# Issuing weight loads from ScalarE in a mixer, and adding half of the experts' rows in the last chunk

## The reference

```python
for l in range(DEPTH):                                   # 2 layers
    sh1, sc1, gt1, sh2, sc2, gt2 = modulation(cond, w_ada[l], b_ada[l])   # cond @ w_ada (1024 x 6144)
    h   = adaln(x, norm_attn[l], sh1, sc1)
    mix = mixer(h)      # windowed attention | bidirectional gated DeltaNet, then one output projection
    x   = residual(x, gt1, mix)
    x   = residual(x, gt2, routed_moe(adaln(x, norm_ffn[l], sh2, sc2)))   # 16 experts, 2 per token
```

## Time and profile before

| | us |
|---|---|
| median of 3 runs | 1897.55 |
| lowest, highest | 1893.96, 1897.66 |
| the profiled execution, its own time | 1897.15 |
| its span, first to last instruction | 1895.4 |
| PE busy | 1631.1 (86%) |
| DVE, ACT, POOL busy | 1207.6, 932.4, 242.2 |
| mean granted clock of TensorE | 0.932 |

### The profile page before, as it was taken

The page is one execution under the profiler, slowest core; times in us unless marked ns, Lnnn a source line. Parts: engine busy times, 40 slices in busy tenths (PEclk is TensorE's granted clock), DMA queues, the critical chain, the costliest instruction groups (busy, mean ns, idle before and its releaser), DMA issues. The chain is left out here.

```text
span 1895.4 us, 32729 instructions
## 1 busy us (share of the span) xinstructions
PE 1631.1 (86%) x11909; PEld 1325.4 (70%) x11910; DVE 1207.6 (64%) x1728; ACT 932.4 (49%) x1438; POOL 242.2 (13%) x361
## 2 busy tenths in 40 slices
PE   3998886799895999999949989789979679999992
PEld 0798675687553888888838986678855468888881
DVE  1478453556346996996664883646654579899664
ACT  2254642233323886886543445323341278888651
POOL 0000035111000111111020000541200011111112
PEclk7899998999896999999969999879999889999996
DMA  8241356654305997997553110665331489999754
GB/s 339 78 151 48 100 153 163 189 178 143 137 34 205 412 405 294 380 408 269 211 218 112 56 48 1 174 197 157 95 129 53 167 304 402 408 397 409 296 198 178
DMA packets 186803, 392.96 MB, mean 207 GB/s; under 512 B 88682, under 2 KB 106114, under 8 KB 161094
## 3 DMA queue, kind: packets, MB, share of 16 engines
q1 hardware_dynamic: 163374, 326.12, 47.7%
q10 hardware_dynamic: 14824, 34.39, 4.6%
q0 software_dynamic: 8496, 30.94, 4.3%
HBM read 345.95 MB, written 45.45 MB: 207 GB/s over the span
## 5 line engine op out<-in xcount | busy, mean ns | idle before, releaser
L2363 DVE TENSOR_TENSOR expert_w_lo<-shared,expert_w_hi 128x2048 fp32r<-128x2048 f32 x192 | 433.4, 2287 | 58.3 <-ACT expert_w_hi L2302 58.3
L2302 ACT ACTIVATE expert_w_hi<-shared 128x2048 fp32r<-128x2048 f32 x192 | 366.5, 1913 | 44.1 <-PEq L146 39.6
L2229 PE MATMUL ps<-expert_w_hi,expert_x_hi 128*128 128x512 f32 x592 | 245.2, 414 | 11.0 <-DVE expert_x_lo L2358 9.2
L2231 PE MATMUL ps<-expert_w_hi,expert_x_lo 128*128 128x512 f32 x592 | 233.2, 394 | 0.0
L2230 PE MATMUL ps<-expert_w_lo,expert_x_hi 128*128 128x512 f32 x592 | 233.1, 394 | 0.0
L2229 PEld LDWEIGHTS ps<-expert_w_hi,expert_x_hi 128*128 128x128 f32 x592 | 113.5, 192 | 42.5 <-issue 12.9
L2231 PEld LDWEIGHTS ps<-expert_w_hi,expert_x_lo 128*128 128x128 f32 x592 | 112.3, 190 | 24.3
L2230 PEld LDWEIGHTS ps<-expert_w_lo,expert_x_hi 128*128 128x128 f32 x592 | 112.8, 191 | 18.7
L2284 PE MATMUL ps<-expert_w_hi,expert_hid_hi 128*128 128x512 f32 x296 | 115.8, 391 | 0.5 <-ACT expert_hid_hi L2337 0.5
L2199 POOL COPY expert_cur_idx<-slot_tokens 128x1 int32 x37 | 48.4, 1307 | 530.2 <-PE ps L2216 530.2
L2285 PE MATMUL ps<-expert_w_lo,expert_hid_hi 128*128 128x512 f32 x296 | 115.3, 390 | 0.0
(11 more groups left out here) (380 smaller groups left out, 3376.7 us busy)
## 6 DMA issues: line engine op xcount, KB each, us to landing
shared<-in_w_up SPq DMA_DIRECT2D x64, 1024.0 KB, 7.4
shared<-in_w_down SPq DMA_DIRECT2D x64, 1024.0 KB, 9.4
shared<-in_w_gate SPq DMA_DIRECT2D x64, 1024.0 KB, 8.3
qkv<-in_w_ada SPq DMA_DIRECT2D x20, 1280.0 KB, 6.1
shared<-in_w_in SPq DMA_DIRECT2D x10, 2048.0 KB, 9.2
y_table<-expert_y ACTq DMA_DIRECT2D x37, 512.0 KB, 8.5
qkvT<-in_w_ada SPq DMA_DIRECT2D x20, 768.0 KB, 8.5
setup_ada_ring<-in_w_ada SPq DMA_DIRECT2D x8, 1024.0 KB, 12.2
```

Of the source, the lines that this page charges most:

```text
L2229: pe.matmul(bank, x_hi[:, at], w_hi[:, j, w], start=(q == 0), stop=False)
L2231: return pe.matmul(bank, x_lo[:, at], w_hi[:, j, w], start=False, stop=(q == KD - 1))
L2302: act.activation(w_hi[:, j, :], raw[:, j, :], ACT.Copy).then_inc(w_hi_done, 1)
L2363: dve.tensor_tensor(w_lo[:, j, :], raw[:, j, :], w_hi[:, j, :].bitcast(F32), ALU.subtract).then_inc(w_lo_done, 1)
```

## The change

Three things change.

- `load_after` moves from SP's order to ACT's: it now stands behind the two exponentials of a pair (`exps`). The wait for `done` and both issues of the load move with it. With it goes the place of `scatter(0)`, `x_load(0)` and `y_load(0)`, which now stand ahead of `base_load(3)`.
- The tables are laid out anew. `base_x` and `base_y` are written in the order in which steps read them, so that a step loads X and Y in 2 DMAs each of 128 KB, not 4 of 64 KB. The corner and the scores' tables get one entry for each tile and direction, and a step loads each in one DMA, not two. Each corner store writes two entries of 64 rows.
- The rows of slot 0 are gathered and added in the last chunk of the experts' phase (`FirstHalf`): in layer 0 for tiles 0 and 1 (into piece 5 of the weights' raw buffer), in the last layer gathered for all five tiles and added for tiles 0 and 1; tiles 2 to 4 are added at the head of `combine_phase`. POOL starts these gathers once the last piece is split and all y stores but the last have landed. `Joined` gathers for tiles 0 and 1 only slot 1, and ACT does nothing for them. The gate row is now loaded ahead of `load_first`.

```diff
+EARLY = 2
@@ Joined
-            for n in range(2):
+            for n in range(int(t < EARLY), 2):
...
+        if t < EARLY:
+            dve.wait_ge(self.got[t], 16)
+            dve.scalar_tensor_tensor(out=b, in0=b, scalar=w, in1=g, op0=ALU.mult, op1=ALU.mult).then_inc(self.gated, 1)
+        else:
...
+class FirstHalf:
+    def gathers(self, pool):
+        for t in self.tiles:
+            pool.indirect_dma_start(out=self.rows[:, t, :], out_offset=None, in_=self.A.y_table,
+                                    in_offset=bass.IndirectOffsetOnAxis(ap=self.R.slots[:, 0, t:t + 1], axis=0)).then_inc(self.got[t], 16)
+
+    def dve_sum(self, dve, t):
+        G, a = self.G, self.rows[:, t, :]
+        dve.wait_ge(self.got[t], 16)
+        dve.scalar_tensor_tensor(out=a, in0=a, scalar=self.R.gates[:, 0, t:t + 1], in1=G.gate_view[:, int(t > 0), :],
+                                 op0=ALU.mult, op1=ALU.mult).then_inc(self.scaled, 1)
+        dve.wait_ge(self.scaled, t + 1)
+        dve.tensor_tensor(G.x[:, t, :], G.x[:, t, :], a, ALU.add).then_inc(self.summed, 1)
@@ projection_phase, ACT
-                    for t in range(2):
-                        joined.act_first(act, t)
@@ mixer_phase, SP
-                        sp.dma_start(A.corner[i], flat(BtLF[i])).then_inc(s_["bl_out"], 16)
+                        sp.dma_start(mine(A.corner, i, HB * DH * HB).rearrange("f (r n) -> f r n", r=HB), flat(BtLF[i])).then_inc(s_["bl_out"], 16)
...
-                    for d in range(2):
-                        sp.dma_start(flat(BtL)[half(d)], A.corner[place(s, d), half(d)]).then_inc(s_["bl_in"], 16)
+                    sp.dma_start(flat(BtL), both(A.corner, s, HB * DH * HB).rearrange("f (r n) -> f r n", r=HB)).then_inc(s_["bl_in"], 16)
...
-                    for d in range(2):
-                        for b in range(2):
-                            sp.dma_start(X[half(b), d], large(A.base_x, place(s, d), b)[:, d * DH:(d + 1) * DH]).then_inc(s_["xy_in"], 16)
+                    for b in range(2):
+                        sp.dma_start(eight_of(X, b), large(entry(A.base_x, 2 * s, 2), b)).then_inc(s_["xy_in"], 16)
...
                     if i + 1 < FRONT:
                         front_out(i + 1)
+                        if i == 2:
+                            scatter(0)
+                            x_load(0)
+                            y_load(0)
                         base_load(i + 1)
-                    units.load_after(sp, i)
-                    if i == 2:
-                        scatter(0)
-                        x_load(0)
-                        y_load(0)
                     units.store_after(sp, i)
                 for s in range(NT):
                     m = FRONT + PER * s
-                    units.load_after(sp, m)
...
-                    units.load_after(sp, m + 1)
...
-                    units.load_after(sp, m + 2)
@@ mixer_phase, ACT, exps(n)
                     ins.then_inc(s_["exp_done"], 1)
+                    units.load_after(act, n)
@@ expert_phase, SP
-                if l + 1 < DEPTH:
-                    sp.wait_ge(w_lo_done, (NE - 1) * PIECES + 4)
-                    load_first(sp, A, G, l + 1, True, True)
                 sp.wait_ge(w_lo_done, (NE - 1) * PIECES + 5)
                 sp.dma_start(G.gate_view, A.mod_rows[l][:, 5 * D:6 * D].partition_broadcast(P)).then_inc(G.gate_in, 16)
+                if l + 1 < DEPTH:
+                    load_first(sp, A, G, l + 1, True, True)
@@ expert_phase, POOL, behind the last chunk
+                pool.wait_ge(w_lo_done, NE * PIECES)
+                pool.sem_inc(passed, 1)
+                pool.wait_ge(y_out, total * 16)
+                pool.sem_inc(passed, 1)
+                half.gathers(pool)
@@ expert_phase, DVE, chunk, ahead of the copy of y
+                    if last and final:
+                        dve.wait_ge(G.gate_in, 16 * (l + 1))
+                        for t in range(EARLY):
+                            half.dve_sum(dve, t)
@@ combine_phase, DVE
                 dve.wait_ge(G.gate_in, 16 * (l + 1))
+                for t in range(EARLY, NT):
+                    first_half(t)
                 for t in range(NT):
...
+                    second_half(t)
```

More of the change, by code:

```diff
@@ L50 @@
 NB = P // SB
-BASE = 2 * 4 * 2 * (HB * HB + HB)
+BASE = 4 * 2 * (HB * HB + HB)
 BASE_PAD = 11 * P * 256
@@ L413, in dve_sum, with __init__ @@
         dve.wait_ge(self.gated, t + 1)
         dve.tensor_tensor(G.x[:, t, :], G.x[:, t, :], b, ALU.add).then_inc(self.added, 1)
+class FirstHalf:
+    def __init__(self, ph, G, A, l, R):
+        self.G, self.A, self.R = G, A, R
+        self.tiles = range(EARLY if l + 1 < DEPTH else NT)
+        at = 5 * PIECE if l + 1 < DEPTH else 0
+        self.rows = G.carve(at, (len(self.tiles), D))
+        self.got = [ph.dma_sem(G.soft[f"y_early{t}"]) for t in self.tiles]
+        self.scaled, self.summed = ph.sem("early_scaled"), ph.sem("early_summed")
+    def gathers(self, pool):
[9 more added lines that the diff above has]
+        dve.tensor_tensor(G.x[:, t, :], G.x[:, t, :], a, ALU.add).then_inc(self.summed, 1)
@@ L1108, in tiles @@
             return (0, 0) if s == 0 else (s, NT - s)
-        def place(s, d):
-            return ORDER.index(tiles(s)[d])
         def at(s, d):
@@ L2409, in combine_phase @@
         ph = Phase(nc, ctx, "combine", l)
-        yy = ph.sb("yy", [P, NT, 2, D])
-        gate = G.gate_view
+        yy = ph.sb("yy", [P, NT, D])
+        late = G.carve(0, (NT, D))
         got = [ph.dma_sem(G.soft[f"y_got{t}"]) for t in range(NT)]
-        first, both, gated, added, x_out = (ph.sem(n) for n in ("first", "both", "gated", "added", "x_out"))
+        scaled, summed, gated, added, x_out = (ph.sem(n) for n in ("late_scaled", "late_summed", "gated", "added", "x_out"))
         with nc.Block() as block:
@@ L2430, in _ @@
                 for t in range(NT):
-                    pool.wait_ge(got[t], 32)
-            @block.scalar
-            def _(act):
-                for t in range(NT):
-                    act.wait_ge(got[t], 32)
-                    act.activation(yy[:, t, 0, :], yy[:, t, 0, :], ACT.Copy, scale=R.gates[:, 0, t:t + 1]).then_inc(first, 1)
+                    pool.wait_ge(got[t], 16)
             @block.vector
             def _(dve):
+                gate = lambda t: G.gate_view[:, int(t > 0), :]
```

113 lines of the change are left out of this document (67 added, 46 removed).

## The result

The changed kernel takes 1871.08 us (median of 4 runs, 1868.3 to 1872.01) against 1897.61 us for the kernel before on the same chip (4 runs, 1893.96 to 1899.37): a ratio of 0.9872, 95% interval 0.9855 to 0.9889. The ratios in this text are estimates from all the runs, and differ from the quotient of the two medians, here 0.9860, by up to 0.0012 (2 us). The profiled execution took 1870.73 us, its span is 1868.7 us (before 1897.15 and 1895.4).

What follows compares the result with a forecast made beforehand. TensorE's own order, with its gaps, was taken to bound the mixers. Mixer gains of 11.3 and 11.7 us, 23.0 cut to 19.5, plus 2.3 at the seam and 7.2 at the end, made 29.0: 1868 us, range 1857 to 1883.

Steps and rivals of the forecast that it cites:

- Part A: 18 of 20 weight loads move from SP to ACT: fewer TensorE waits in both mixers, less some new ones.
- part B: SP's fewer issues and new order end the wait before step 0: 7.7 us in layer 0, 7.9 in layer 1.
- part C: First slot's rows gathered and added in the last chunk: 2.3 us gained at the layers' seam, 7.2 at the end.
- The prediction's own sign of being wrong: TensorE's idle time in the mixers falls by less than 12 us, or y's last-chunk copy starts over 3 us later.
- A, waits that go: Layer 0's mixer: weight waits at pairs 3, 5 and 10 vanish, with faster products behind pair 10: 12.1 us.
- A, three loads at 2.5 us each: Layer 0: ACT reaches the exponentials of pairs 10, 13 and 16 only in the next step, costing 7.5 us.
- A, ScalarE in the way: TensorE waits for ACT, delayed by load issues, in 5 places: 1.0 us in layer 0, 0.5 in layer 1.
- A, 85%: Of the mixers' 23.0 us only 85%, 19.5, counted, since DVE and ACT also caught up in TensorE's gaps.
- B, no wait before step 0: Y lands at 289.8, before TensorE's 291: 6.9 us go in layer 0, 7.7 with slow products; 7.9 in layer 1.
- The rule for a DMA's engines: Corner store would run on 2 engines, X(0) some 3 us later per layer; forecast then 1870 to 1874.
- half-of-the-mixers case: Rival, 17%: slow corner stores, late loads and ACT's issues leave 4 us in layer 0, 8 in layer 1; 1877.
- The forecast's own case: The whole kernel at 1862 to 1874 us, given 55%.

Runs made afterwards that it cites:

- experiment 2: The kernel before with only the first slot's rows gathered and added in the last chunk, mixers untouched: 1886.85 us, ratio 0.995.
- experiment 3: The changed kernel with its weight loads back on SyncE at their old places in the loop: 1891.06 us, ratio 0.9969.
- experiment 6: The kernel before with only the corner table padded, so each corner store has two or four groups of rows: 1907.92 us in two, 1900.19 us in four.

## Why the prediction was right, and where it was not

The total is right by luck, by errors that cancel. Part A was forecast at 3.6 + 3.8 = 7.4 us (6.3 at 85%) and gave 17; part B at 15.6 us (13.3) and cost some 3.6; part C was right. The prediction's own sign of being wrong came true besides: TensorE's idle time in the mixers fell by 6.7 us, not by 12 or more (by 11.8 if the mixers of experiment 2's execution are taken as those before). Of the 32.0 us that the sum counts as gained in the mixers (12.1 + 7.7 + 4.3 + 7.9) it puts under 5 down to faster products; measured, they were 8 to 10 of 17 to 20. Point by point:

- **A, waits that go.** Right. Part A alone takes them from 16.2 to 5.1 us in layer 0, and from step 0 on TensorE is busy 157.9 us instead of 160.3: 13.5 us for the two, and I had 12.1. Pair 17's 0.7 us, which I let stay, went too.
- **A, three loads at 2.5 us each.** Wrong, and the largest error in part A: 0.4 us with A alone, 1.0 in the changed kernel. I took the issue to start behind the exponentials, whose end stands 2.9 us behind the products both before (381.63 to 384.58) and now (374.31 to 377.25). It starts 1.1 us behind the products (375.45), beside the engine's work.
- **A, ScalarE in the way.** 1.0 us expected; TensorE's waits for ScalarE's `pT` copy are 2.2 us from step 0 on, with A as before: in layer 0 no cost shows.
- **A, 85%.** Wrong in sign: the waits for DVE's scores fell too, from 12.0 to 8.9 us from step 0 on. A alone gave layer 0 17.3 us, not 3.6. In layer 1 it gave 3.9, and the forecast was 3.8, but that too is a sum of two: 6.3 us gained from step 0 on, 2.4 lost ahead of it.
- **B, no wait before step 0.** Wrong. I gave it 7.7 and 7.9 us; against the mixers of C alone, B made layer 0's 1.6 us longer and layer 1's 0.6 shorter. The step that failed is "the landing (some 1.4)" of the scatters, which took 7.2 us beside a weight load, and with it the corner store ("I cost it at nothing"). (In experiment 3, with every load on SP, they land in 2.3 us, but their issues run from 284.85 to 291.81, where 2.1 us were forecast.) In two groups of rows the store costs 12.9 us in the kernel before and 13.5 in the changed one. Split, B gives 6.1 us in layer 1 (216.2 to 210.1) and nothing in layer 0 (222.9 to 224.2), where the weight loads' company takes it.
- **The rule for a DMA's engines.** By the Trainium skill (DMA: Bandwidth & Descriptors, "Why a DMA increments its semaphore by 16 and not by 1") I had put the forecast at 1870 to 1874 and the price at 3 us a layer. The counts of experiment 6 agree with the rule. That 1871 lies in that range is luck as well: the price was 13 us in two layers and not 6.
- **C.** The end is exact: y's copy loses nothing, and 7.3 us are gained. At the seam y comes 1.9 us late as forecast, but only 2.8 us come back instead of 4.35: ScalarE's first step of the next phase begins 5.5 us after the store of y (949.37 to 954.85), before 4.2, so DVE is busy with splits until 961.8 and can't begin the sums earlier. Why ScalarE begins 1.3 us later the runs do not show.
- **Rivals.** The half-of-the-mixers case had one true cause, corner stores that hold SP's front back, and put the gain at 4 and 8 us; it was 12.4 and 4.3. The forecast's own case (1862 to 1874) came true in its number alone. Transfers did not speed up in the front part, they slowed down. ScalarE's two issues took 0.91 us in most loads: no block.
- **Stated tests.** The wait before step 0, the three new waits, the 22 us at the seam (23.3) and the 12 us of idle time failed; the issues, the end and the place of y's copy (1.9 us late, under 3) held, and pair 10's wait went but for 1.25 us.

## What to carry to other kernels

A sum can be right while two terms of it are off by 10 us and more each, in opposite directions; stage times at fixed places of the program show it, and a run with each part alone tells whose they are. When a layout changes, look at what the slowest dimension of each transfer becomes: a store cut to two groups of rows cost 13 us here, and splitting it in two issues won that back. A bulk load moved to a second queue no longer blocks the first one's program order, but it still flies beside the first one's small tables, which then come up to 7 us later.

## What was not expected of the hardware

- A DMA's issue on ScalarE's queue started before the engine ran the exponentials that stand ahead of it in the program: 375.45 against 375.71 to 377.25.
- A 128 KB store in 2 groups of rows is waited for by SP for 6.8 us in one layer's front part, in 4 groups 1.7 us, as 128 rows 0.5 us (L986 in the kernel before). For the forms in groups the profile's view of issues gives no time to landing; the increments in the trace do: 2.3 us after the start of the issue as 128 rows, 3.7 in four groups, 5.0 in two. Beside a weight load the same three took 8.0, 9.2 and 10.0 us.
- The four scatters of 32 KB each have landed 1.4 us after their last issue in the kernel before, and after 6.5 to 7.3 us where a 2 MB load left during them on the other queue; with rows of 512 bytes in that load, after 3.65.
- Idle time costs twice. The first 40 products of pair 10 take 1.30 us behind a wait of 1.25 us, at a granted clock of 1.00 (2.4 GHz), and took 2.36 behind one of 7.35, at 0.50 (1.2 GHz). The length of the last wait alone does not decide it: behind 2.58 us pair 5 ran at 1.00 before, behind 2.31 us pair 6 ran at 0.55 in the changed kernel.
